# Conformer convolution: GpSimd writes the low part's diagonal of four of the thirteen taps that TensorE multiplies

## The chip, the cores and the metric

The kernel runs on one core of a Trainium2 chip. The metric is the device time of one execution in microseconds (us): 984.08 us is the median of three runs before the change (983.99 to 984.74). TensorE (PE, with its weight loads as PEld), VectorE (DVE), ScalarE (ACT), GpSimd (POOL) and SyncE (SP) each run their own instruction stream, and semaphores order them against each other.

## What is computed

Three transformer blocks stand one after the other on a sequence of 256 tokens of 1024 channels, in float32: a block with softmax attention, one with differential attention, both with a gated feed-forward network behind them, and then a Conformer block with a gated feed-forward network that has a short convolution of its own. The change lies in the Conformer's convolution module, which the reference writes as

```python
u = h @ w1 + b1
a, gt = jnp.split(u, 2, axis=-1)
u = a * jax.nn.sigmoid(gt)
u = causal_dwconv(u, dw_w) + dw_b      # 31 taps, one weight per tap and channel
u = jax.nn.silu(layernorm(u, ln_g, ln_b))
return u @ w2 + b2
```

## The kernel before

Every product on TensorE is made of three matmuls of rounded parts: a value is split into a high part (rounded to the fp32r format) and a low part (what is left), and high x high, high x low and low x high are added up in PSUM. ACT writes the high parts of weights (`prep`, line 1009), DVE the low parts (`prep`, line 1351).

The kernel has six stages `s`, and the Conformer's mixer is stage 4, from about 664 to 780 us of the span. It loops over eight blocks `T` of 128 channels (`step(i, j)` with T = 2i + j, on each engine). For one block PE makes two column products of 24 matmuls each (`col_product`, line 537), for `a` and the gate; ACT takes the sigmoid of the gate (line 1268); DVE multiplies the two into the padded row `upad` (line 1775); ACT writes its high part `u_hi` (line 1279) and DVE its low part `u_lo` (line 1768).

The 31 taps of the convolution are shared. DVE does 18 of them itself, one instruction each over 256 tokens with the tap's weights as a scalar per channel, in two running sums (lines 1791, 1794 or 1796, and 16 of line 1799), and adds the two sums into `part` (line 1806). PE does the other 13 (`NP`) in `conv(T)` (line 893): a tap is a multiplication by a 128 x 128 matrix that has the tap's weights on its diagonal, three matmuls a tap: high diagonal x `u_hi`, high diagonal x `u_lo`, low diagonal x `u_hi`. `combine(T)` on DVE (line 1757) adds PE's sum and `part` into `convT`. PE runs `conv(T-1)` behind the column products of block T. The last block's convolution stands alone behind that of the block before it.

The diagonals are written by ACT (`diags`, line 1255): the identity matrix times a column of `taps`, two instructions a tap, the high one into `diag[0]` and the low one into `diag[1]`, 26 a block. There is one set of buffers, so the diagonal of tap m for block T is written once `conv(T-1)` has multiplied tap m (`diag_used`), and `conv(T)` waits for it tap by tap (`diag_done`).

POOL has little to do in this stage: for each block it gathers the block's 31 tap weights, three biases and 26 split weights into a small tile (`channel_taps(T)`, lines 451, 453, 455), once DVE is done with the block two before; at blocks 4 and 5 it also takes a mean off four finished blocks (`centred`, line 512). POOL's instructions run in the order of its program, and a wait holds up all that stand behind it.

Of the kernel before, what the change touches and what calls it, by code (L numbers as in the profile page):

```python
# [33 lines left out]
NP = 13  # L34
# [22 lines left out]
STEPS = {1: 0, 3: 22, 4: 44, 5: 52}  # L57
HEADS = {0: 0, 2: 8}
GATE_BANK = {0: 1, 1: 0, 2: 2, 3: 0, 4: 0, 5: 0}
NI_A, NI_F, NI_C = H // 2, FT // 2, KT // 2  # L60


def build(nc, x, c, rel_bias, ada_w, ada_b, norm_g, moba_w_qkv, moba_w_o, diff_w_qkv, diff_w_o,
# [4 lines left out]
    with ExitStack() as ctx:  # L68
# [3 lines left out]
        def sem(name):  # L72
            return ctx.enter_context(nc.semaphore(name))
# [152 lines left out]
        pad_zero, tap_seq, conv_done = sem("pad_zero"), sem("tap_seq"), sem("conv_done")  # L226
        thi, tlo = sem("taps_hi_done"), sem("taps_lo_done")
        uhi, ulo = sem("u_hi_done"), sem("u_lo_done")
        diag_done, diag_used, part_done = sem("diag_done"), sem("diag_multiplied"), sem("part_done")
        mean_mm, d_done = sem("mean_mm"), sem("d_done")  # L230
        sq_done, var_mm, lms_done, lrs_done = sem("sq_done"), sem("var_mm"), sem("lms_done"), sem("lrs_done")
# [183 lines left out]
        @block.gpsimd  # L415
        def _(pool):
            def row(src):

                return bass.AP(src.tensor, src.offset, [[0, P], [1, D]])

            def acc_init(n, layer, lo_c, hi_c):

                for at in range(lo_c, hi_c, D):
                    pool.memset(acc[:, at:at + D], 0.0).then_inc(acc_zero, 1)
                pool.wait_ge(acc_zero, 6 * ((n - 1) // 2) + hi_c // D - FIRST)
                bias = ada_b[layer:layer + 1, lo_c:hi_c] if layer < 2 else mod_b_2[0:1, lo_c:hi_c]
                pool.dma_start(acc[0:1, lo_c:hi_c], bias).then_inc(acc_bias[n - 1], 16)

            def gains(layer):
                need(pool, x_ready, 4 * layer)  # L430
                post = ((norm_g[layer, 1], norm_g[layer, 3]) if layer < 2
                        else (norm_post_mix_2[0], norm_post_ffn_2[0]))
                for g, src in zip((Ga, Gf), post):
                    pool.dma_start(g[:], row(src)).then_inc(gain_loaded, 16)
                if layer == 2:
                    pool.dma_start(b2full, row(a_pw2_b_2[0])).then_inc(b2_loaded, 16)

            def rstd_y(s, t):

                c = slice(t, t + 1)  # L440
                pool.wait_ge(msy_done, 2 * s + t + 1)
                pool.tensor_tensor(rsy[:, c], msy[:, c], mhalf, ALU.pow).then_inc(rsy_done, 1)  # L442

            def channel_taps(T, j):

                if T > 1:
                    pool.wait_ge(part_done, T - 1)
                    pool.wait_ge(diag_done, T * NP - NP)
                adw = cols[:, ADW:ADW + CONV * KT].rearrange("p (c t) -> p c t", t=KT)
                bias = cols[:, PW1B:PW1B + 3 * KT].rearrange("p (c t) -> p c t", t=KT)  # L450
                pool.tensor_scalar(taps[j][:, 0:CONV].rearrange("p (c t) -> p c t", t=1),
                                   adw[:, :, T:T + 1], 1.0, None, ALU.mult).then_inc(taps_ready, 1)
                pool.tensor_scalar(taps[j][:, CONV:CONV + 3].rearrange("p (c t) -> p c t", t=1),
                                   bias[:, :, T:T + 1], 1.0, None, ALU.mult).then_inc(taps_ready, 1)
                pool.tensor_scalar(taps[j][:, 36:36 + 2 * NP].rearrange("p (t w c) -> p t w c", t=1, w=2),
                                   tap_parts[:, T:T + 1, :, :], 1.0, None, ALU.mult).then_inc(taps_ready, 1)

            pool.memset(ident[:], 0.0).then_inc(id_zero, 1)
            pool.wait_ge(id_zero, 1)
            pool.affine_select(out=ident[:], in_=ident[:], compare_op=ALU.not_equal, fill=1.0, base=0,  # L460
                               pattern=[[-1, P]], channel_multiplier=1).then_inc(consts, 1)
            pool.memset(ones[:], 1.0).then_inc(consts, 1)
            pool.memset(mhalf, -0.5).then_inc(consts, 1)
            pool.memset(per_channel, 1.0 / D).then_inc(consts, 1)
            pool.memset(xt_eps[:, :, D:D + 1], (D * EPS) ** 0.5).then_inc(consts, 1)
            acc_init(2, 0, 2 * D, 6 * D)
            pool.wait_ge(consts, 5)
            for s in range(LAST + 1):
                for t in range(TT):
                    pool.wait_ge(ssx_done, 2 * s + t + 1)  # L470
                    pool.tensor_tensor(rsx[:, t:t + 1], ssx[:, t:t + 1], mhalf, ALU.pow).then_inc(rsx_done, 1)
                if s in (2, 4):
                    pool.wait_ge(mod_gf, s // 2)
                    pool.wait_ge(hlo, h_parts_before(s + 1))
                    acc_init(s + 2, s // 2, 5 * D, 6 * D)
                    gains(s // 2)
                elif s in (1, 3):
                    pool.wait_ge(mod_ga, s // 2 + 1)
                    pool.wait_ge(mod_cols, s + 1)
                    pool.wait_ge(hlo, h_parts_before(s + 1))  # L480
                    acc_init(s + 2, s // 2 + 1, 0, 5 * D)
                if s == 0:
                    pool.wait_ge(rel_row, 1)
                    pool.dma_start(rel_small, relrow).then_inc(rel_stored, 16)
                    pool.wait_ge(rel_stored, 16)
                    pool.wait_ge(ld[3], 16)
                    for lo_c, hi_c in ((0, 2 * P), (2 * P, 3 * P)):
                        src = bass.AP(rel_small.tensor, rel_small.offset + 1, [[1, P], [REL, H], [1, hi_c - lo_c]])
                        pool.dma_start(head_bias[:, :, lo_c:hi_c], src).then_inc(bias_loaded, 16)
                    gains(0)  # L490
                if s == 1:
                    pool.wait_ge(lam_seq, 2)
                    pool.memset(oraw_eps[:, :, P:P + 1], 8 * (2 * EPS) ** 0.5).then_inc(eps_column, 1)
                if s == 2:
                    def head_rstd(i):
                        for at in range(2 * TT):
                            t = at % TT
                            pool.wait_ge(oss, i * 4 + at + 1)
                            pool.tensor_tensor(rso[:, t:t + 1], sso[:, t:t + 1], mhalf, ALU.pow)\
                                .then_inc(ors, 1)  # L500
                    with pool.Fori(0, NI_A) as i:
                        head_rstd(i)
                if s == 3:
                    pool.wait_ge(cols_ready, 2)
                    pool.wait_ge(tlo, 1)
                    for T in range(2):
                        channel_taps(T, T)
                if s == 4:
                    def centred(k):
                        pool.wait_ge(shift_done, 1)  # L510
                        pool.wait_ge(conv_done, k + 1)
                        pool.tensor_tensor(convT[:, k, :], convT[:, k, :], shift, ALU.subtract).then_inc(sub_done, 1)

                    for T in range(2, KT):
                        channel_taps(T, T % 2)
                        if T == 4:
                            for k in range(3):
                                centred(k)
                        if T == 5:
                            centred(3)  # L520
                    pool.wait_ge(lms_done, 1)
                    pool.tensor_tensor(ln_rs, ln_ms, mhalf.broadcast_to([P, TT]), ALU.pow).then_inc(lrs_done, 1)
                for t in range(TT):
                    rstd_y(s, t)
# [3 lines left out]
        def _(pe):  # L528
# [353 lines left out]
            def conformer():  # L882
                nb, fb = USE[4][0], STEPS[4]

                def conv(i, j, half_way=None):
# [3 lines left out]
                    need(pe, conv_done, T - 1)  # L889
                    for m in range(NP):  # L890
                        pe.wait_ge(diag_done, T * NP + (m + 1))
                        for n, (w, u) in enumerate(((0, u_hi), (0, u_lo), (1, u_hi))):
                            mm = pe.matmul(Y[:, j, 0:S], diag[w][:, m, :], u[j][:, m:m + S],
                                           start=(m == 0 and n == 0), stop=(m == NP - 1 and n == 2))
                        mm.then_inc(diag_used, 1)
                        if half_way and m == NP // 2:
                            half_way()
# [106 lines left out]
        def _(act):  # L1004
# [235 lines left out]
            def conformer():  # L1240
# [4 lines left out]
                def step(i, j, more):  # L1245
# [4 lines left out]
                    def diags(m0, m1):  # L1250
                        for m in range(m0, m1):
                            if not (start and j == 0):
                                act.wait_ge(diag_used, T * NP + (m + 1 - NP))
                            for w in range(2):
                                d = act.activation(diag[w][:, m, :], ident[:], ACT.Copy,  # L1255
                                                   scale=taps[j][:, 36 + w * NP + m:37 + w * NP + m])
                            d.then_inc(diag_done, 1)
# [694 lines left out]
```

## Time and profile before

| | |
|---|---|
| median of three runs | 984.08 us (983.99 to 984.74) |
| the profiled execution | 984.03 us, of which the span is 982.2 us |
| busy share of the span | PE 96%, PEld 88%, DVE 84%, ACT 55%, POOL 8% |
| granted TensorE clock | 0.993 of full speed over the span |
| Conformer loop, eight blocks | about 667 to 753 us of the span |

Busy is the time in which an engine had an instruction in flight. Instructions of one engine overlap a little (the next starts before the last result has landed), so the distance from start to start says more of an engine's pace than a single duration.

### The profile page before, as it was taken

The numbers are of one execution on the slowest core, as the hardware profiler recorded it, in microseconds if no ns is written. First come the engines' busy times: TensorE is split into PE (matmuls) and PEld (weight loads), VectorE is DVE, ScalarE is ACT, GpSimd is POOL, SyncE is SP. The second block draws the span as 40 slices with busy tenths as digits, with TensorE's granted clock in tenths as the row PEclk, the third lists the DMA queues.
The fourth block names the chain that finished last, engine by engine and source line by source line (L and its number), as shares of the span: only waits on it lengthen the run. The fifth ranks groups of instructions, "written<-read, shape, count | busy, mean of one in ns | idle before, by whom it ended". The sixth has DMA issues, their size and how long they took to land. (4 is left out here: it accounts for less than half of the span.)

```text
span 982.2 us, 19019 instructions
## 1 busy us (share of the span) xinstructions
PE 947.5 (96%) x6806; PEld 868.6 (88%) x6806; DVE 820.6 (84%) x1217; ACT 544.3 (55%) x1023; POOL 78.0 (8%) x111
## 2 busy tenths in 40 slices
PE   4899999999999999998999999999999999999997
PEld 3899988999999888996999999989997899999996
DVE  4869988898888778777888888889998979988885
ACT  3465546454444566555554444459998555555552
POOL 2100002000000011111300000002240000000000
PEclk9899999999999999999999999999999999999999
DMA  9999983999999965652599999986340549766641
GB/s 347 328 329 349 336 278 97 349 350 343 303 333 322 279 193 162 183 174 84 166 348 359 321 322 317 318 267 173 87 129 1 181 134 301 220 196 192 190 127 43
DMA packets 240770, 234.08 MB, mean 238 GB/s; under 512 B 7497, under 2 KB 208970, under 8 KB 240714
## 3 DMA queue, kind: packets, MB, share of 16 engines
q1 hardware_dynamic: 237824, 226.52, 73.7%
q0 software_dynamic: 1616, 5.32, 1.7%
q10 hardware_dynamic: 1274, 1.52, 0.5%
q8 instruction: 31, 0.51, 0.2%
q14 instruction: 25, 0.20, 0.1%
HBM read 232.27 MB, written 1.06 MB: 238 GB/s over the span
## 5 line engine op out<-in xcount | busy, mean ns | idle before, releaser
L537 PE MATMUL work<-h_hi,whi_a 128*128 128x256 f32 x1360 | 379.0, 279 | 2.8 <-DVE h_lo L1412 2.8
L537 PE MATMUL work<-h_lo,whi_a 128*128 128x256 f32 x1360 | 377.4, 277 | 0.0
L537 PE MATMUL work<-h_hi,wlo_a 128*128 128x256 f32 x1360 | 377.3, 277 | 0.0
L1351 DVE TENSOR_TENSOR wlo_a<-raw,whi_a 128x1024 fp32r<-128x1024 f32 x180 | 218.6, 1223 | 52.2 <-ACT whi_a L1009 51.8
L537 PEld LDWEIGHTS work<-h_hi,whi_a 128*128 128x128 f32 x1360 | 256.3, 188 | 6.4 <-issue 2.9
L537 PEld LDWEIGHTS work<-h_lo,whi_a 128*128 128x128 f32 x1360 | 256.8, 189 | 2.7
L537 PEld LDWEIGHTS work<-h_hi,wlo_a 128*128 128x128 f32 x1360 | 256.4, 189 | 0.0
L1009 ACT ACTIVATE whi_a<-raw 128x1024 fp32r<-128x1024 f32 x180 | 187.9, 1054 | 61.1 <-PE work L537 38.3
L1361 DVE SCALAR_TENSOR_TENSOR acc<-ada_raw,csil,acc 128x1024 f32 (+1 forms) x128 | 163.5, 1279 | 7.2 <-DMA ada_raw<-in_ada_w 5.6
L1009 ACT ACTIVATE whi_b<-raw 128x1024 fp32r<-128x1024 f32 x106 | 110.7, 1055 | 81.4 <-DMA raw<-in_ffn_w_out 42.8
L1351 DVE TENSOR_TENSOR wlo_b<-raw,whi_b 128x1024 fp32r<-128x1024 f32 x106 | 128.5, 1219 | 8.8 <-ACT whi_b L1009 8.6
L574 PE MATMUL Y<-whi_b,ab_hi 128*128 128x512 f32 x286 | 89.9, 395 | 1.1 <-DVE ab_lo L1661 1.1
L574 PE MATMUL Y<-wlo_b,ab_hi 128*128 128x512 f32 x286 | 89.9, 395 | 0.0
L574 PE MATMUL Y<-whi_b,ab_lo 128*128 128x512 f32 x286 | 89.7, 395 | 0.0
L574 PEld LDWEIGHTS Y<-whi_b,ab_lo 128*128 128x128 f32 x286 | 53.7, 188 | 13.0
L574 PEld LDWEIGHTS Y<-wlo_b,ab_hi 128*128 128x128 f32 x286 | 53.7, 188 | 12.3
L442 POOL TENSOR_TENSOR small<-small 128x1 f32<-128x1 f32 x12 | 6.6, 552 | 674.8 <-DVE small L1462 674.8
L574 PEld LDWEIGHTS Y<-whi_b,ab_hi 128*128 128x128 f32 x286 | 49.0, 188 | 8.8 <-issue 1.2
L1799 DVE SCALAR_TENSOR_TENSOR mix<-mix,taps 128x256 f32<-128x256 f32 x128 | 51.3, 476 | 0.0
L1230 ACT ACTIVATE ab_hi<-mix 128x256 fp32r<-128x256 f32 x66 | 27.1, 411 | 33.3 <-DVE mix L1700 17.8
L1221 ACT ACTIVATE mix<-work 128x256 f32<-128x256 f32 x44 | 16.7, 379 | 43.1 <-PE work L537 43.1
L1255 ACT ACTIVATE wlo_b<-ident,taps 128x128 fp32r<-128x128 f32 x104 | 40.4, 389 | 0.0
(228 smaller groups left out, 1395.6 us busy)
## 6 DMA issues: line engine op xcount, KB each, us to landing
ada_raw<-in_ada_w SPq DMA_DIRECT2D x88, 512.0 KB, 6.4
raw<-in_ffn_w_in SPq DMA_DIRECT2D x88, 512.0 KB, 7.9
ada_raw<-in_mod_w SPq DMA_DIRECT2D x48, 512.0 KB, 6.8
raw<-in_ffn_w_out SPq DMA_DIRECT2D x44, 512.0 KB, 6.2
raw<-in_f_up_w SPq DMA_DIRECT2D x44, 512.0 KB, 4.3
raw<-in_moba_w_qkv SPq DMA_DIRECT2D x24, 512.0 KB, 8.4
raw<-in_diff_w_qkv SPq DMA_DIRECT2D x24, 512.0 KB, 8.0
raw<-in_a_pw_w SPq DMA_DIRECT2D x24, 512.0 KB, 7.4
```

Of the source, the lines that this page charges most:

```text
L442: pool.tensor_tensor(rsy[:, c], msy[:, c], mhalf, ALU.pow).then_inc(rsy_done, 1)
L537: mm = pe.matmul(dst, w[u][:, ws], h[:, k, :], start=(k == 0 and m == 0), stop=(k == KT - 1 and m == 2))
L574: mm = pe.matmul(Y[:, 2 * t + f, :], a[:, ts], w[u][:, f * 512:(f + 1) * 512], start=(first and m == 0), stop=False)
L1009: act.activation(whi[u], raw[:, u, :], ACT.Copy).then_inc(hi[u], 1)
L1221: act.activation(gate[:, j, :], work[:, 2 * j, 0:S], ACT.Silu).then_inc(gate_done, 1)
L1230: act.activation(a_hi[j], act32[:, j, :], ACT.Copy).then_inc(ahi, 1)
L1255: d = act.activation(diag[w][:, m, :], ident[:], ACT.Copy, scale=taps[j][:, 36 + w * NP + m:37 + w * NP + m])
L1351: dve.tensor_tensor(wlo[u], raw[:, u, :], whi[u].bitcast(F32), ALU.subtract).then_inc(lo[u], 1)
L1361: dve.scalar_tensor_tensor(at, ada_raw[:, q % 4, :], csil[:, ccol:ccol + 1], at, ALU.mult, ALU.add).then_inc(gemv, 1)
L1799: v = dve.scalar_tensor_tensor(sums, u[:, m:m + S], w, sums, ALU.mult, ALU.add)
```

## The change

A new function `low_diagonals(T)` on POOL writes `diag[1]`, the low diagonal, of taps 6, 8, 10 and 12 with one `tensor_scalar` each: identity times a column of `taps`, 128 x 128, into the fp32r buffer. ACT leaves these four out, so it writes 22 diagonals a block in place of 26. PE waits for a further semaphore ahead of these four taps. On POOL, the diagonals of blocks 0 and 1 stand at the stage's start, and those of a later block right behind its `channel_taps`; each waits for `conv(T-1)` to have multiplied the same tap, as ACT's do. All other instructions and their orders stay.

```diff
+POOL_TAPS = (6, 8, 10, 12)
...
+            def low_diagonals(T):
+
+                pool.wait_ge(taps_ready, 3 * T + 3)
+                for m in POOL_TAPS:
+                    if T:
+                        pool.wait_ge(diag_used, T * NP + (m + 1 - NP))
+                    tap = 36 + NP + m
+                    pool.tensor_scalar(diag[1][:, m, :], ident[:], taps[T % 2][:, tap:tap + 1], None,
+                                       ALU.mult).then_inc(low_diag_done, 1)
...
+                    for j in range(2):
+                        pool.wait_ge(used[6 + j], USE[4][3])
+                        low_diagonals(j)
                     for T in range(2, KT):
                         channel_taps(T, T % 2)
+                        low_diagonals(T)
...
                     for m in range(NP):
                         pe.wait_ge(diag_done, T * NP + (m + 1))
+                        if m in POOL_TAPS:
+                            pe.wait_ge(low_diag_done, T * len(POOL_TAPS) + POOL_TAPS.index(m) + 1)
...
-                            for w in range(2):
+                            for w in range(1 if m in POOL_TAPS else 2):
                                 d = act.activation(diag[w][:, m, :], ident[:], ACT.Copy,
                                                    scale=taps[j][:, 36 + w * NP + m:37 + w * NP + m])
```

## Rows read from the trace of the kernel before

**Rows 1.** Busy time by stretch: PE, PEld, DVE, ACT, POOL, clock, DMA.

```profile
688.71:699.41 10.70, 10.70 (x90) 10.51 (x90) 10.70 (x25) 10.33 (x31) 2.80 (x3) 1.00 0.34 100
...
710.11:722.00 11.89, 11.89 (x101) 11.67 (x100) 11.89 (x26) 11.78 (x33) 4.95 (x7) 1.00 0.31 90
```

**Rows 2.** Timeline of DVE, block 2: start, duration, line, tiles, count.

```profile
690.25 1.22 DVE L1351 TENSOR_TENSOR wlo_a<-raw,whi_a 128x1024 fp32r<-128x1024 f32 x1
691.38 0.46 DVE L1768 TENSOR_TENSOR ab_lo<-mix,ab_hi 128x286 fp32r<-128x286 f32 x1
691.76 0.40 DVE L1791 TENSOR_SCALAR mix<-mix,taps 128x256 f32<-128x256 f32 x1
...
692.34 6.41 DVE L1799 SCALAR_TENSOR_TENSOR mix<-mix,taps 128x256 f32<-128x256 f32 x16
698.68 0.41 DVE L1757 TENSOR_TENSOR head_bias<-Y,xs 128x256 f32<-128x256 f32 x1
699.01 0.41 DVE L1806 TENSOR_TENSOR xs<-mix 128x256 f32<-128x256 f32 x1
```

**Rows 3.** Waits, 660 to 765 us: total, times, longest.

```profile
ACT ab_hi L1279 <- DVE mix L1775: 4.4, 5, 1.6
PEld Y L893 <- ACT wlo_b L1255: 3.0, 17, 0.2
```

**Rows 4.** Timeline of ACT, block 2: first and last of 26 diagonals.

```profile
690.71 0.39 ACT L1255 ACTIVATE whi_b<-ident,taps 128x128 fp32r<-128x128 f32 x1
...
698.03 0.40 ACT L1255 ACTIVATE wlo_b<-ident,taps 128x128 fp32r<-128x128 f32 x1
```

**Rows 5.** Busy time by stretch, line 893 alone (conv of blocks 1 and 2).

```profile
681.90:688.20 6.30, 6.26 (x39) 5.09 (x39) 1.00 0.45 128
694.40:699.00 4.60, 4.56 (x39) 4.60 (x39) 1.00 0.30 89
```

**Rows 6.** Timeline of POOL, 688 to 700 us.

```profile
688.80 1.32 POOL L451 TENSOR_SCALAR taps<-cols 128x31 f32<-128x31 f32 x1 [7.89 <-DVE xs L1806]
...
690.29 1.32 POOL L455 TENSOR_SCALAR taps<-head_bias 128x26 f32<-128x26 f32 x1
```

**Rows 7.** Timeline of POOL, 710 to 715.9 us.

```profile
710.79 3.74 POOL L512 TENSOR_TENSOR head_bias<-head_bias,xs 128x256 f32<-128x256 f32 x3 [8.48 <-ACT xs L1272]
...
715.13 0.50 POOL L455 TENSOR_SCALAR taps<-head_bias 128x26 f32<-128x26 f32 x1
```

**Rows 8.** Timeline of DVE, the same stretch and its end.

```profile
711.69 1.33 DVE L1351 TENSOR_TENSOR wlo_a<-raw,whi_a 128x1024 fp32r<-128x1024 f32 x1
712.94 0.98 DVE L1768 TENSOR_TENSOR ab_lo<-mix,ab_hi 128x286 fp32r<-128x286 f32 x1
713.85 0.83 DVE L1791 TENSOR_SCALAR mix<-mix,taps 128x256 f32<-128x256 f32 x1
...
715.00 6.41 DVE L1799 SCALAR_TENSOR_TENSOR mix<-mix,taps 128x256 f32<-128x256 f32 x16
```

**Rows 9.** Timeline of POOL and of DVE at 481.6 us (stage 3).

```profile
481.57 0.28 POOL L455 TENSOR_SCALAR taps<-head_bias 128x26 f32<-128x26 f32 x1
...
481.61 1.29 DVE L1361 SCALAR_TENSOR_TENSOR acc<-ada_raw,csil,acc 128x1024 f32<-128x1024 f32 x1
```

**Rows 10.** Line 1361: count, duration in ns (least, median, most).

```profile
L1361 DVE SCALAR_TENSOR_TENSOR acc<-ada_raw,csil,acc x128: 1272/1278/1335, 64.4 to 866.0; 128x1024 f32<-128x1024 f32 x64, 128x1024 f32 x64
```

**Rows 11.** Groups by line of POOL: busy us, mean ns.

```profile
L424 POOL MEMSET acc<- 128x1024 f32 x16 | 14.6, 957 | 26.9 <-DVE h_lo L1412 26.9
...
L458 POOL MEMSET ident<- 128x128 f32 x1 | 0.2, 206 | 0.3 <-POOLq L1941 0.3
```

**Rows 12.** Timelines of ACT, PE and DVE at the loop's end.

```profile
750.57 0.39 ACT L1255 ACTIVATE wlo_b<-ident,taps 128x128 fp32r<-128x128 f32 x1
...
751.70 0.28 PE L893 MATMUL Y<-ab_hi,wlo_b 128*128 128x256 f32 x1
...
752.10 0.43 DVE L1806 TENSOR_TENSOR xs<-mix 128x256 f32<-128x256 f32 x1
```

More of the change, by code:

```diff
@@ L228, in build @@
         uhi, ulo = sem("u_hi_done"), sem("u_lo_done")
+        low_diag_done = sem("low_diag_done")
         diag_done, diag_used, part_done = sem("diag_done"), sem("diag_multiplied"), sem("part_done")
```

## The prediction

> **What bounds the kernel now.** I read the busy time by stretch first, with one stretch for each block of the Conformer loop, then DVE's timeline of one block, then the waits, and only then the page's list of costly groups, because the change touches one loop and a share over the whole span says little about it.
>
> The reader is to see in the stretches that DVE is busy for all of the 10.70 us of a block, and that PE and nearly ACT (10.33 us) look full as well [rows 1]. Three full engines can't all be the bound, so the question is who waits for whom. In the waits, ACT stands still for 4.4 us in five places until DVE has made its product of line 1775, and PE stands still for 3.0 us in 17 short pieces until ACT has written a low diagonal [rows 3]. DVE waits for nobody: its timeline goes from one instruction to the next with no gap from the start of the loop to the last block [rows 2], and no wait of DVE stands in that list between 678 and 753 us. PE's fullness is partly pacing: the same 39 matmuls take 6.26 us in one block and 4.56 us in another [rows 5]. So DVE sets the length of a block, ACT is ahead of it, and PE has room. At the loop's end it is the same: ACT starts its last diagonal at 750.57 and PE its last matmul of the convolution at 751.70, but DVE starts the sum that `combine` needs only at 752.10 [rows 12].
>
> **What is removed.** ACT's 26 diagonals of a block start at an even pace, the first at 690.71 and the last at 698.03 [rows 4]: 7.32 us over 25 steps, 0.293 us each. Four fewer free 4 x 0.293 = 1.17 us a block, 9.4 us over eight blocks. I cost this at nothing: what hides it is DVE's block of 10.70 us. ACT comes to its next high part of u 1.17 us earlier and waits that much longer there for DVE; the 4.4 us of [rows 3] grow by up to 1.17 us a block. PE gets its diagonals earlier, and its next stop is DVE's product of the block before (`act_done`), which is not earlier. If DVE had a wait that the trace hides, the 3.0 us of PE's waits would be what there is to win (a rival below).
>
> **What is added on POOL, and whether it comes too late.** There are 32 new instructions, four a block. The trace has none of this shape. One of 26 elements takes 0.28 us where DVE hardly stands against it [rows 9], and three two-input instructions of 256 elements took 3.74 us, 1.25 each, amid DVE's work [rows 7]. Four therefore take between 1.1 and 5.0 us. POOL has 7.89 us of idle time ahead of a block's taps [rows 6]. The diagonals of block T become possible while `conv(T-1)` runs; for T = 3 that is up to 699.0 [rows 5], and `conv(3)` starts one pair of column products behind that, over 5 us later, with tap 6 two us into it. The taps of the block after are gathered behind the new instructions: those at 688.80 to 691.6 [rows 6] are first read in the DVE block from 699.41 on [rows 1], so they have nearly 8 us of slack. I cost lateness at nothing; without that slack, each us that POOL is late would stop PE for one.
>
> **What it costs DVE.** This term decides. POOL and DVE hold each other up in this trace. A POOL instruction of 31 elements that starts with a low part of 128 x 1024 (1.22 us, as in [rows 2]) takes 1.32 us and ends just behind it, and another of 26 elements does the same [rows 6]. The other way round, while POOL took the mean off three blocks [rows 7], DVE's instructions at 712.94 and 713.85 took 0.98 and 0.83 us [rows 8] where the same ones take 0.46 and 0.40 [rows 2]: 0.52 and 0.43 us lost to one POOL instruction each, and 0.11 at 711.69. Together these 1.06 us are, with 0.13 for a dearer form of the second tap, the difference between the 11.89 us of that block and 10.70 [rows 1].
>
> The new instructions are smaller, read one tensor, and fall mostly within the 16 taps of line 1799. Bounds for one of them:
> - Below: nothing. POOL's 26 elements at 715.13 ran inside those 16 taps, which took 6.41 us [rows 7, 8], as without them [rows 2]. Room for that is visible: the taps start every 0.396 us (6.34 us from 692.34 to 698.68, by 16), while a DVE element costs 1.04 ns (1.13 us from 690.25 to 691.38 for 1024 elements less 0.33 from 698.68 to 699.01 for 256, over 768 [rows 2]), so 256 elements stream for 0.27 us and 0.13 us of each tap streams nothing.
> - Above: half of the 0.475 that a 256-wide POOL instruction cost on the mean, 0.24 us. A gain from POOL's side is excluded: POOL takes no work off DVE.
> - Nearest row: 26 POOL elements that met a DVE instruction head on cost it 0.01 us (1.29 against the median of 1.278) [rows 9, 10]. A POOL element costs 0.84 ns (957 less 206 ns over 896 elements [rows 11]), so 102 more cost 0.086 us: 0.10 if the 26 had just filled the free time. If they had not, 128 elements x 0.84 = 0.11 us still fit into the 0.13 and cost nothing.
>
> I take 0.07 us, nearer to the 0.10 than to nothing, for the 28 instructions of blocks 1 to 7. The four of block 0 stand among the 1024-wide low parts, which leave only 1.13 - 1024 x 1.04 ns = 0.07 us free; for them I take 0.12. The Trainium skill, page "SBUF — State Buffer", section "Who interferes with whom", speaks against the change: a DVE instruction with two SBUF inputs and a GpSimd instruction that reads SBUF exclude each other, and whoever started first holds the port for its whole instruction. The trace agrees on the exclusion [rows 6, 8], but 0.50 us of POOL within the taps at no cost to them [rows 7, 8] speaks against the "whole". By that rule the sum would be that of the third rival, by the rows it is the following.
>
> **The sum.** 28 x 0.07 = 2.0 and 4 x 0.12 = 0.5, together 2.4 us more; 0 gained on ACT and PE; nothing behind the loop, since `combine` of the last block moves with DVE. The profiled execution took 984.03 us (its span 982.2 and 1.8 around it), 0.05 under the median of 984.08. So 984.08 + 2.4 = 986.5 us, slower by 0.25%. A measurement of this kernel can tell about 0.2% (2.0 us) from no change.
>
> **The rivals.**
> 1. *It all fits into DVE's free time.* The new instructions cost 0 to 0.03 us each, under 1 us together: 984.1 to 985. For it speaks the tap chain that did not stretch; against it the 0.43 to 0.52 us of the larger instructions, and that five times as many elements are read as in the one that fitted. Chance 0.25.
> 2. *ACT, not DVE, paces the loop: faster.* If DVE's unbroken chain hides waits for PE's sum, then PE's waits for diagonals (3.0 us in 17) set the end, and 1.17 us a block less on ACT would remove nearly all of them: 984.1 - 3.0 = 981.1. It decides from the point where PE's sum of a block comes later than DVE's own part. For it speaks that `conv` is stretched from 4.56 to 6.26 us by ACT's pace [rows 5]; against it that ACT itself waits for DVE in five of eight blocks and that a DVE block is 10.70 us whether `conv` took 6.26 or 4.56. Chance 0.07.
> 3. *POOL holds DVE for all of its instruction.* One of 128 elements lasts some 0.28 + 0.09 = 0.37 us alone; less the 0.13 that the taps leave free, 0.24 each, 32 x 0.24 = 7.7: 991.8. The rule named above would give this. For it speaks that 0.43 to 0.52 us is about the whole of a larger instruction; against it the taps that did not stretch [rows 7, 8]. Chance 0.11.
> 4. *POOL is starved by the 16 taps* and its diagonals come only in the low parts behind them, so that PE or the next taps wait: a us or two in each of some blocks, around 990. Against it speaks that POOL's 26 elements got through the taps in 0.50 us. Chance 0.02.
>
> **How the numbers follow.** My forecast, 0.03 to 0.13 us for each instruction, has the remaining 0.55 and covers 985 to 988.3; of it about 0.15 lies under +2.0 us. Faster by over 0.2%: rival 2, 0.07. Within 0.2%: rival 1 and that part of the forecast, 0.25 + 0.15 = 0.40. Slower: 0.40 + 0.11 + 0.02 = 0.53. The range reaches from rival 1 to 0.17 us an instruction (32 x 0.17 = 5.4): 984.0 to 989.5. It leaves out rival 2 and the upper part of rival 3, some 0.17.
>
> **What the profile after would show.** Right: 22 diagonals of ACT and four POOL instructions of 128 x 128 a block; ACT's wait for line 1775 grown by about a us a block; PE's waits for ACT's diagonals nearly gone; DVE still without a gap, its block 2 at about 11.0 us in place of 10.70, the 16 taps at about 6.7 in place of 6.41, single taps lengthened where a POOL instruction starts. Wrong: the 16 taps still at 6.41 (rival 1); a block under 10.70 (rival 2); 16 taps at 7.2 or more (rival 3); a wait of PE for a POOL instruction, or of DVE or ACT for the gathered taps (rival 4).

## The result, and the profile after

The changed kernel takes 987.66 us (median of 11 runs, 985.62 to 989.52) against 984.26 for the kernel before (11 runs, 983.25 to 986.13): a ratio of 1.0029, interval 1.0018 to 1.0039, or 2.9 us (1.8 to 3.8) more. The two medians lie 3.4 us apart; the ratio is estimated from all the runs of both kernels. The forecast was 2.4 us more.

The waits of the changed kernel from 660 to 770 us (total, times, longest) answer to [rows 3]:

```profile
ACT ab_hi L1297 <- DVE mix L1793: 14.1, 7, 4.0
...
PEld Y L911 <- ACT wlo_b L1273: 1.0, 6, 0.2
```

ACT's wait for DVE's product (now line 1793) has grown from 4.4 to 14.1 us: the 9.4 us taken off ACT became waiting, as forecast, and 0.3 more. PE's waits for ACT's diagonals fell from 3.0 to 1.0 us, and nothing came of that either. No wait of PE for a diagonal of POOL is listed. In the groups by line one sees the work itself, 72 low diagonals on ACT (104 before) and 32 on POOL:

```profile
L467 POOL TENSOR_SCALAR wlo_b<-ident,taps 128x128 fp32r<-128x128 f32 x32 | 44.8, 1415 | 20.4 <-PE Y L911 20.3
...
L1273 ACT ACTIVATE wlo_b<-ident,taps 128x128 fp32r<-128x128 f32 x72 | 27.9, 388 | 0.0
```

A diagonal takes ACT 0.39 us and POOL 1.4 on the mean. DVE is still without a gap, and seven of its eight blocks are longer. Busy time by stretch, blocks 2, 4 and 5 (columns as in [rows 1]):

```profile
689.79:700.65 10.86, 10.78 (x90) 10.52 (x90) 10.86 (x25) 9.29 (x27) 7.50 (x8) 1.00 0.36 98
711.52:724.11 12.59, 12.59 (x109) 12.54 (x108) 12.59 (x26) 9.33 (x27) 11.57 (x14) 1.00 0.29 84
724.11:735.41 11.30, 10.00 (x70) 8.59 (x70) 11.30 (x26) 9.12 (x26) 7.37 (x6) 1.00 0.57 187
```

Block 2 is 0.16 us longer, block 4 is 0.70 [rows 1], and block 5 is 0.34 (10.96 before). DVE's timeline tells where; line 1817 is the former 1799, the 16 taps, here of blocks 1, 2 and 4:

```profile
682.78 6.41 DVE L1817 SCALAR_TENSOR_TENSOR mix<-mix,taps 128x256 f32<-128x256 f32 x16
...
693.48 6.58 DVE L1817 SCALAR_TENSOR_TENSOR mix<-mix,taps 128x256 f32<-128x256 f32 x16
...
715.33 8.19 DVE L1817 SCALAR_TENSOR_TENSOR mix<-mix,taps 128x256 f32<-128x256 f32 x16
```

Block 1's taps are as long as before, block 2's 0.17 and block 4's 1.78 us longer. POOL's timeline says why. First the four diagonals for block 2, then one of those for block 5:

```profile
685.97 3.70 POOL L467 TENSOR_SCALAR wlo_b<-ident,taps 128x128 fp32r<-128x128 f32 x1 [3.92 <-PE Y L911]
...
689.66 1.82 POOL L467 TENSOR_SCALAR wlo_b<-ident,taps 128x128 fp32r<-128x128 f32 x1
...
691.46 1.96 POOL L467 TENSOR_SCALAR wlo_b<-ident,taps 128x128 fp32r<-128x128 f32 x1
...
693.40 0.63 POOL L467 TENSOR_SCALAR wlo_b<-ident,taps 128x128 fp32r<-128x128 f32 x1
...
720.59 0.84 POOL L467 TENSOR_SCALAR wlo_b<-ident,taps 128x128 fp32r<-128x128 f32 x1
```

The first one started at 685.97 among block 1's taps and, by its end, got nothing done until these were over: it ended at 689.67, just behind `combine` (line 1775, from 689.12), one of whose two inputs lies in PSUM. The next two ended with the product that reads PSUM (line 1793, from 690.92) and with the first tap, which reads one tensor (line 1809, from 692.82), and the fourth at 694.03, within the 16 taps of block 2. In block 4 it was otherwise: a diagonal went through every second tap, 0.84 us each, and the taps around it are hardly longer:

```profile
720.56 0.48 DVE L1817 SCALAR_TENSOR_TENSOR mix<-mix,taps 128x256 f32<-128x256 f32 x1
...
720.97 0.50 DVE L1817 SCALAR_TENSOR_TENSOR mix<-mix,taps 128x256 f32<-128x256 f32 x1
...
721.39 0.47 DVE L1817 SCALAR_TENSOR_TENSOR mix<-mix,taps 128x256 f32<-128x256 f32 x1
```

From 720.56 to 721.39 are two taps, 0.83 us in place of 2 x 0.396: 0.04 us for one POOL instruction. What made block 4 long is something that POOL had done before as well, the three subtractions of `centred` (now line 524). The diagonals ahead of them in POOL's order ended at 715.87 and so pushed them out of the stretch of DVE's low parts, 710.8 to 714.5 in [rows 7], into its taps:

```profile
715.85 2.49 POOL L524 TENSOR_TENSOR head_bias<-head_bias,xs 128x256 f32<-128x256 f32 x3
```

```profile
715.84 1.02 DVE L1817 SCALAR_TENSOR_TENSOR mix<-mix,taps 128x256 f32<-128x256 f32 x1
716.79 0.95 DVE L1817 SCALAR_TENSOR_TENSOR mix<-mix,taps 128x256 f32<-128x256 f32 x1
```

There each costs about half a us (0.95 from 715.84 to 716.79, less 0.396). The fourth subtraction was put off as well. It started at 724.00, just ahead of block 5's first low part:

```profile
724.11 1.75 DVE L1369 TENSOR_TENSOR wlo_a<-raw,whi_a 128x1024 fp32r<-128x1024 f32 x1
```

That low part took 1.75 us in place of 1.22. Before, the fourth started at 721.89, and the two low parts beside it took 1.22 and 1.37.

**Where the span went.** The profiled spans differ by 3.8 us: DVE comes to the loop 0.76 later (664.59 against 663.83), the loop takes 2.05 more, the stretch from its end to the first line that adds the mixer to x (30.50 against 29.54) 0.96, all behind that 0.03. The first part lies ahead of anything that was changed. In the third TensorE's granted clock fell to 0.50, the lower of its two levels, while PE did the one-column matmuls of the layer norm's sums, and stayed there longer than before. Busy time by stretch, the clock third from the end:

```profile
759.00:761.00 2.00, 2.00 (x4) 0.89 (x5) 1.55 (x5) 0.51 (x1) 0.72 (x1) 0.50 0.00 0
761.00:763.00 2.00, 2.00 (x7) 1.25 (x6) 0.97 (x4) 0.39 (x1) 0.00 (x0) 0.50 0.00 0
```

The kernel before has such a fall too (0.50 from 758 to 760). The experiments show whether it belongs to the change.

### The profile page after: what moved, and what is told of

It is laid out like the page before. It is cut to its first block and busy times, and to the rows that moved or that the text cites. A ratio compares the mean times of both kernels' runs of the same rounds, so it can differ in the third digit from the quotient of the medians.

```text
span 986.0 us, 19059 instructions
## 1 busy us (share of the span) xinstructions
PE 949.2 (96%) x6806; PEld 870.7 (88%) x6806; DVE 822.7 (83%) x1217; ACT 534.5 (54%) x991; POOL 115.5 (12%) x143
## 3 DMA queue, kind: packets, MB, share of 16 engines
HBM read 232.27 MB, written 1.06 MB: 237 GB/s over the span
## 5 line engine op out<-in xcount | busy, mean ns | idle before, releaser
L1817 DVE SCALAR_TENSOR_TENSOR mix<-mix,taps 128x256 f32<-128x256 f32 x128 | 53.7, 492 | 0.0
L467 POOL TENSOR_SCALAR wlo_b<-ident,taps 128x128 fp32r<-128x128 f32 x32 | 44.8, 1415 | 20.4 <-PE Y L911 20.3
```

Of the source, the lines that this page charges most:

```text
L467: pool.tensor_scalar(diag[1][:, m, :], ident[:], taps[T % 2][:, tap:tap + 1], None, ALU.mult).then_inc(low_diag_done, 1)
L1817: v = dve.scalar_tensor_tensor(sums, u[:, m:m + S], w, sums, ALU.mult, ALU.add)
```

## The experiments

The theory: DVE sets the loop; POOL's instructions that read hold DVE up, by themselves and by pushing `centred` into the taps. Rivals: the other half of the change, ACT's shorter list, moves PE's pace and clock; POOL's waits or any POOL instruction do it; the new instructions cost the same wherever they stand.

A kernel's time scatters by some 3 to 4 us over 11 runs (experiments 6 and 7 have 6), so I also read the loop in each profile, from DVE's first low part of a weight to the start of the last `combine`; the last column is the stretch from there to the line that adds to x. Each of these readings is of one execution; that of experiment 4 was the fastest of its 11 (984.33, median 986.11) and that of experiment 5 the second slowest (986.58, median 985.03). Times are in us.

| kernel | ratio to before (interval) | loop | blocks 0 to 7 | behind |
|---|---|---|---|---|
| before | 1 | 88.80 | 14.18 10.70 10.70 10.70 11.89 10.96 10.75 8.92 | 29.54 |
| the change | 1.0029 (1.0018 to 1.0039) | 90.85 | 14.56 10.64 10.86 10.87 12.59 11.30 10.99 9.04 | 30.50 |
| POOL's work alone | 1.0014 (1.0005 to 1.0023) | 90.86 | 14.51 11.03 10.69 10.81 12.48 11.31 10.99 9.04 | 29.57 |
| ACT's relief alone | 0.9998 (0.9989 to 1.0007) | 88.70 | 14.18 10.64 10.62 11.13 11.51 10.95 10.75 8.92 | 30.48 |
| memsets on POOL | 1.0003 (0.9993 to 1.0013) | 88.84 | 14.20 10.69 10.70 10.70 11.89 10.98 10.76 8.92 | 30.57 |
| `centred` first | 1.0016 (1.0007 to 1.0025) | 89.65 | 14.45 10.63 10.87 11.12 11.60 11.17 10.76 9.05 | 29.53 |
| 14 taps, with POOL | 1.0006 (0.9997 to 1.0014) | 87.72 | 14.17 10.24 10.48 10.47 11.76 10.71 10.36 9.53 | 30.09 |
| 14 taps, without | 1.0040 (1.0028 to 1.0053) | 90.33 | 13.80 11.27 11.29 11.28 11.50 11.27 10.78 9.14 | 30.71 |
| eight taps on POOL | 1.0028 (1.0017 to 1.0040) | 91.60 | 14.79 11.00 10.81 11.98 11.55 11.20 11.00 9.27 | 29.83 |

**1. POOL's work alone.**

```diff
-                    pool.tensor_scalar(diag[1][:, m, :], ident[:], taps[T % 2][:, tap:tap + 1], None,
+                    pool.tensor_scalar(unused[POOL_TAPS.index(m)], ident[:], taps[T % 2][:, tap:tap + 1], None,
...
-                        if m in POOL_TAPS:
-                            pe.wait_ge(low_diag_done, T * len(POOL_TAPS) + POOL_TAPS.index(m) + 1)
...
-                            for w in range(1 if m in POOL_TAPS else 2):
+                            for w in range(2):
```

> GpSimd's 32 new instructions alone: ScalarE writes all 26 diagonals of a block again, TensorE waits for none of GpSimd's, and GpSimd does the same four multiplications a block at the same places into diagonal slots that nobody reads. Theory (VectorE sets the loop and is held up by GpSimd's reads): as slow as the change, +2 to +3.5 us (ratio 1.002 to 1.0035), and the Conformer loop, from the first low part of its weights to the last combine, about 2.0 us longer than before. Rival (the loss comes from the other half of the change, ScalarE's shorter list, which shifts TensorE's pace and its clock behind the loop): within 0.5 us of before.

The loop is 2.06 us longer than before, the change's 2.05 to the hundredth. The time is 1.4 us up (0.5 to 2.3), under the expected 2 to 3.5, and its interval overlaps that of the change. So in the profiles POOL's instructions alone make the whole of the loop's loss, and it doesn't matter whether PE uses their result. In this execution block 1 paid, where the change's did not: three diagonals were still running from 678.64 to 682.81, and of the next four, from 685.68 on, three ran inside the taps. The taps of DVE's timeline:

```profile
682.26 6.78 DVE L1819 SCALAR_TENSOR_TENSOR mix<-mix,taps 128x256 f32<-128x256 f32 x16
```

**2. ACT's relief alone.**

```diff
-                        if m in POOL_TAPS:
-                            pe.wait_ge(low_diag_done, T * len(POOL_TAPS) + POOL_TAPS.index(m) + 1)
...
-                    for j in range(2):
-                        pool.wait_ge(used[6 + j], USE[4][3])
-                        low_diagonals(j)
...
-                        low_diagonals(T)
```

> ScalarE's relief alone: it leaves out the four low diagonals and GpSimd does not write them; the low-part matmuls of these four taps multiply what the buffer happens to hold. Theory: 0 to -0.6 us (ratio 0.9994 to 1.000); the VectorE block 1 at 10.64 us in place of 10.70, since only 0.06 us of each block waited for ScalarE. Rival 2 of the prediction (ScalarE's diagonals pace the loop): -3 us (0.997). Rival (the shorter list shifts the clock behind the loop): +0.6 us or more, with a longer stretch at the low clock.

No change that can be measured, and 0.10 us off the loop. Rival 2 of the prediction, that ACT's diagonals pace the loop, would have given 3 us. ACT's wait for DVE is longer here too:

```profile
ACT ab_hi L1291 <- DVE mix L1787: 12.1, 7, 2.6
```

Blocks 1 and 2 are 0.06 and 0.08 us shorter. That is a wait which the trace of before didn't list: there DVE's first low part of block 2 starts at 688.71, 0.40 us behind line 1806 and 0.03 behind the end of ACT's high part of the same weight (688.68); here and in the change it starts 0.33 behind that line. Blocks 3 and 4 have changed places, 11.13 and 11.51: ACT made the mean earlier, and POOL's subtractions began already at 708.21, at the end of block 3.

**3. Memsets in place of POOL's multiplications.**

```diff
-                    pool.tensor_scalar(unused[POOL_TAPS.index(m)], ident[:], taps[T % 2][:, tap:tap + 1], None,
-                                       ALU.mult).then_inc(low_diag_done, 1)
+                    pool.memset(unused[POOL_TAPS.index(m)].bitcast(F32), 0.0).then_inc(low_diag_done, 1)
```

> As the run with GpSimd's work alone, but its 32 instructions are memsets of the same 128 x 128 slots that nobody reads: they write and read no tensor. Theory that it is GpSimd's reading that meets VectorE's second input: 0 to +0.5 us (ratio 1.000 to 1.0005), the 16 taps at 6.41 us wherever GpSimd falls, no GpSimd instruction of more than 0.3 us. Rival (any GpSimd instruction holds VectorE up, or it is the waits and their order): +2 us (1.002), with taps lengthened where they start.

As before: 1.0003, the loop 0.04 us longer, `centred` back in its old place. The timelines of POOL and of DVE show three of the memsets inside the taps of block 1 and these at 6.41 us:

```profile
684.84 0.21 POOL L469 MEMSET wlo_b<- 128x128 f32 x1 [0.87 <-PE Y L910]
...
686.02 0.20 POOL L469 MEMSET wlo_b<- 128x128 f32 x1 [0.97 <-PE Y L910]
```

```profile
680.38 6.41 DVE L1817 SCALAR_TENSOR_TENSOR mix<-mix,taps 128x256 f32<-128x256 f32 x16
```

The waits, the order and the places were those of experiment 1, the instructions only wrote. So POOL's instructions that read meet DVE and those that only write do not, and they meet it both ways: a memset takes 0.21 us where a multiplication of the same size takes 0.84 or waits 3.70. The times alone do not separate experiments 1 and 3 (their intervals overlap); the loop and the taps do. A memset is also shorter, but that is not the reason. In the kernel before, one of 0.96 us stands beside two low parts of DVE:

```profile
663.70 0.96 POOL L424 MEMSET acc<- 128x1024 f32 x1 [6.63 <-DVE h_lo L1412]
...
663.83 2.36 DVE L1351 TENSOR_TENSOR wlo_b<-raw,whi_b 128x1024 fp32r<-128x1024 f32 x2 [0.26 <-ACT whi_b L1009]
```

Two such low parts take the same 2.36 us at 767.28, where POOL does nothing. No run here has POOL compute without reading, so the computing itself is not excluded by an experiment. The Trainium skill, page "SBUF — State Buffer", section "Who interferes with whom", has this rule: a VectorE instruction with two SBUF inputs contends with a GpSimd instruction that reads SBUF, and not with one that only writes. This case agrees.

**4. `centred` ahead of the diagonals.**

```diff
                         channel_taps(T, T % 2)
-                        low_diagonals(T)
                         if T == 4:
                             for k in range(3):
                                 centred(k)
                         if T == 5:
                             centred(3)
+                        low_diagonals(T)
```

> The change with one order turned round: in blocks 4 and 5 GpSimd takes the mean off the finished blocks ahead of its low diagonals, as it did before the change. Theory that 0.7 us of block 4 and 0.3 of block 5 come from these four instructions being pushed from among VectorE's low parts of weights into its taps: +1.2 to +2.2 us against before (1.0012 to 1.0022), block 4 at about 12.0 us in place of 12.59. Rival (the new instructions cost by themselves wherever they stand): as the change, +2.9 us.

1.0016, and the loop 0.85 us over before in place of 2.05. The subtractions start at 709.25, beside the last instructions of block 3 and the low parts of block 4, and block 4's taps are 1.6 us shorter than in the change:

```profile
709.25 3.30 POOL L524 TENSOR_TENSOR head_bias<-head_bias,xs 128x256 f32<-128x256 f32 x3 [4.90 <-ACT xs L1290]
```

```profile
714.63 6.57 DVE L1817 SCALAR_TENSOR_TENSOR mix<-mix,taps 128x256 f32<-128x256 f32 x16
```

Blocks 3 to 5 together take 33.89 us, 34.76 in the change, 33.55 before: 0.87 us came back. The rest of the 1.20, 0.33, stands in blocks 0 and 6 (0.11 and 0.23), whose code is the same in both; why is not shown. By the times alone this run is not separable from the change (1.0016 and 1.0029 with intervals that overlap), and it is no faster than experiment 1, whose subtractions are late too (1.0014). The loop separates them, by one profile each.

**5 and 6. A fourteenth tap on TensorE**, with POOL's diagonals (on top of experiment 4) and without (on top of the kernel before).

```diff
-NP = 13
+NP = 14
```

> The variant with the mean taken off first, and 14 taps on TensorE in place of 13 (17 on VectorE). If VectorE is the bound, one tap less takes 0.396 us off each block, 3.2 us off the loop, until TensorE binds: 48 column matmuls at 0.113 and 42 of the convolution at 0.119 us are 10.4 us a block, 10.75 with a mean's sum. Expected: blocks 1 to 3 at 10.4 to 10.75 us, the loop at 86.5 to 88.3 us against 88.80 before, the time 0.5 to 2.3 us under before (ratio 0.9977 to 0.9995). Rival (GpSimd's eating into VectorE leaves nothing, or TensorE binds fully): 0 to +1 us.

The loop is the shortest of all, 1.08 us under before and as expected, and blocks 1 to 3 (10.24 to 10.48) show that PE doesn't bind at 10.75. But the time is that of before (1.0006), not the 0.5 to 2.3 us under it that I expected; it falls in the rival's range, though neither of the rival's reasons holds. The last block is 0.61 us longer than before, since nothing hides PE's longer sum there; DVE's timeline has the waits in brackets:

```profile
745.01 0.42 DVE L1775 TENSOR_TENSOR head_bias<-Y,xs 128x256 f32<-128x256 f32 x1 [0.68 <-PE Y L911]
...
753.39 0.42 DVE L1775 TENSOR_TENSOR head_bias<-Y,xs 128x256 f32<-128x256 f32 x1 [0.48 <-PE Y L911]
```

The profiled execution lost the rest outside the loop: 1.84 us ahead of it and 0.55 behind. Other kernels here came to the loop between 662.55 and 664.59, this one at 665.67. Experiment 6, with 14 taps too, came at 663.86. Whether experiment 5 tends to come late stays open.

> The kernel before with 14 taps on TensorE and all 28 diagonals on ScalarE. ScalarE then has 28 x 0.293 + 2 x 0.95 + 0.35 + 0.35 = 10.8 us a block, over VectorE's 10.3. Theory: ScalarE becomes the bound, blocks 1 to 3 at 10.8 us, 0 to +1.5 us against before (1.000 to 1.0015), with waits of VectorE or TensorE for ScalarE. Rival (ScalarE has more room than that): as the run with GpSimd's help or better, 1 to 3 us under before.

Slower by 3.9 us, more than expected: blocks 1 to 3 are at 11.3, not 10.8. ACT is the bound: DVE, which waited for nobody, now waits for its high parts.

```profile
DVE wlo_a L1351 <- ACT whi_a L1009: 3.5, 4, 1.0
```

The loop makes 1.5 of the 3.9 us; in the profiled execution another 1.2 stand behind it (30.71 against 29.54). So POOL's help is worth 2.6 us of loop where ACT has 28 diagonals to write; where it has 26, it costs 0.85 (experiment 4, the same order on POOL).

**7. Eight taps on POOL**, in the order of experiment 4.

```diff
-POOL_TAPS = (6, 8, 10, 12)
+POOL_TAPS = (5, 6, 7, 8, 9, 10, 11, 12)
```

> The variant with the mean taken off first, with eight taps (5 to 12) on GpSimd in place of four: twice as many GpSimd multiplications. Theory (each costs VectorE some 0.03 us, 0.85 for 32): the loop at 90.3 to 90.8 us against 89.65 with four, the time 0.7 to 1.2 us above that of four taps. Rivals: GpSimd comes too late and TensorE waits for it, 3 us or more above; or the cost is not one by the instruction, and the loop stays within 0.3 us of that of four taps.

1.0028, 1.2 us over four taps, but the loop is 1.95 over them, not 0.7 to 1.2. ACT waits for the taps that POOL now gathers late, behind the diagonals:

```profile
ACT mix L1286 <- POOL taps L457: 6.7, 4, 2.5
```

That is not what lengthened the loop: in it DVE has no listed wait over 0.2 us. The subtractions met the taps again. Their mean comes from ACT, which has still less to do and made it earlier against DVE's block, so they started in block 3's last taps, and those 16 taps took 7.69 us:

```profile
709.37 0.79 POOL L524 TENSOR_TENSOR head_bias<-head_bias,xs 128x256 f32<-128x256 f32 x1 [0.86 <-ACT xs L1290]
```

```profile
703.63 7.69 DVE L1817 SCALAR_TENSOR_TENSOR mix<-mix,taps 128x256 f32<-128x256 f32 x16
```

Blocks 3 and 4 together are 0.81 us over experiment 4. The other six are 1.14 over it, for 32 more diagonals 0.036 each, near the 0.03 expected. That split is read from one profile each and was not isolated.

**The stretch behind the loop** takes 29.5 us in three profiles (before, experiments 1 and 4) and 30.5 in three others (the change, 2 and 3), whether the time went up or not; experiments 5 to 7 have 30.1, 30.7 and 29.8. In experiment 2, as in the change, the clock stays low for longer, at 0.50 up to 760, nearly 9 us behind the last `combine`. Its busy time by stretch:

```profile
756.00:758.00 2.00, 2.00 (x7) 1.45 (x6) 0.97 (x3) 0.00 (x0) 0.33 (x1) 0.50 0.00 0
758.00:760.00 2.00, 1.65 (x3) 0.24 (x2) 1.81 (x5) 1.73 (x4) 0.00 (x0) 0.50 0.00 0
```

So the 0.96 us of the changed kernel's profile are not shown to belong to the change; single executions fall to either side. 2.05 us of loop agree with the measured 1.8 to 3.8; where the rest of the 2.9 comes from, if it is more than scatter, stays open.

## Why the prediction was right, by its steps

- *DVE is the bound, and 1.17 us a block off ACT is worth nothing*: right. Experiment 2 isolates it, 0.10 us off the loop; DVE's blocks hid a wait for ACT after all, of 0.06 us, so "DVE waits for nobody" was not quite so.
- *POOL's instructions lengthen DVE's chain*: right. Experiment 1 puts the loop's whole loss on them, experiment 3 on their reading.
- *0.07 us for each, 0.12 in block 0*: too dear. Experiment 4 leaves 0.85 us for 32, 0.027 each; in the taps one costs 0.04, below the 0.07 taken. The 0.10 of the working assumed that the 26 elements just filled the free time; they did not. Nor did most diagonals run in the taps, as the working had it: they waited for instructions of DVE that read at most one tensor from SBUF. There they cost little: the four for block 2 cost 0.25 us, 0.08 at line 1809 and the one behind it and 0.17 in the first two taps, where the fourth of them and the gathered taps behind it ran.
- *Lateness costs nothing*: this step failed. It named the gathered taps as what stands behind the new instructions on POOL and left out `centred`, which stands there too, and it took 1.1 to 5.0 us for four diagonals where the trace shows up to 8.3. The four subtractions were not awaited by anyone in time to matter, as the step reckoned; but later meant among other instructions of DVE, at 0.5 us each, where before the first three cost 1.06 together [rows 8] and the fourth 0.15. By these lines that is about 0.8 us more; experiment 4 gives 0.87 us for it in blocks 3 to 5, up to 1.2 in the loop.
- *The sum*, 2.4 us, came out near the loop's 2.05 because the two errors have opposite signs: by experiment 4, 1.5 too much for the diagonals and 0.9 to 1.2 missing for `centred`. That the sum is so near is luck; that the change is slower by some us, on DVE's chain, is not.
- *The rivals*: the second fails by experiment 2. The first and the third fail too (0 to 0.03 each is right for the diagonals alone, but not for the whole; 0.24 is far off). The fourth has half of its mechanism right: 20 of the 32 diagonals came behind the 16 taps that shut out the first of their four. But PE and the taps of the next block waited for none of them, and its 990 did not come.
- *What the profile would show*: block 2 was to be at 11.0 us and its taps at 6.7; they are at 10.86 and 6.58. Its sign of the third rival, 16 taps at 7.2 us or more, came in block 4 (8.19), but from the subtractions.

## What to carry to other kernels

Ask first whether the engine that is relieved is the one that others wait for: ACT's own wait for DVE, in the trace before, said that its work was worth nothing. POOL is not free beside a DVE that never rests: an instruction of POOL that reads holds up DVE's instructions with two SBUF inputs and is held up by them, while one that only writes is not. And when work is put into a queue, list everything behind it and ask what it will run beside when it comes later, not only who waits for it.

## What was not expected of the hardware

A POOL instruction that reads can be shut out by a chain of DVE instructions for as long as the chain lasts: that of 685.97 waited through eight taps of 0.396 us, 3.70 in all. Others went through every second tap in 0.84 us, in the same program, in blocks 0 and 4 of the change. Where DVE reads at most one tensor from SBUF one takes 0.60 us (at 746.93), not the 0.37 that I had estimated. What decides between being shut out and getting in, I did not try, and it stays open. The five profiles with these diagonals have one lead, POOL's idle time just before. For block 1's diagonals in the change, which got in, it was 2.48 us:

```profile
674.65 1.21 POOL L467 TENSOR_SCALAR wlo_b<-ident,taps 128x128 fp32r<-128x128 f32 x1 [2.48 <-PE Y L911]
```

Of the first diagonals of a set that started among taps after such a pause, the nine with 0.10 to 2.48 us got in, and the 16 with 2.85 to 5.73 us ended 0.44 to 0.56 us behind the start of the first instruction that follows the taps; two more started within half a us of that and tell nothing. The two go together in this one program; no run tested it. Whether a diagonal gets in makes single blocks differ by some 0.3 us (block 1: 10.64 in the change, 11.03 with POOL's work alone).
